# The prompt attention of a hybrid decoder: where the second 512 keys of the next step's scores stand in the order of work

## The reference, cut to what matters

```
logits = einsum(q, k_sel) * hd**-0.5          # 8 query heads, 2 KV heads, hd 64
logits = where(valid, logits, -inf)
p = softmax(logits, axis=-1)
o = einsum(p, v_sel)
```

## Time and profile before

| | us |
|---|---|
| median of 3 runs (lowest, highest) | 3653.49 (3647.55, 3655.58) |
| the profiled execution's own time | 3684.45 |
| its span | 3682.6 |
| TensorE busy | 3211.0 (87%) |
| VectorE busy | 1595.3 (43%) |
| ScalarE busy | 1179.6 (32%) |
| prompt attention, first layer | from about 730 to 905 |
| prompt attention, second layer | from about 2512 to 2687 |

### The profile page before, as it was taken

How to read it: one execution, slowest core, us unless ns; L and a number is a source line. 1 busy time by engine, 2 the same in 40 slices (tenths; PEclk the granted TensorE clock), 3 DMA queues, 4 the chain that set the end, 5 groups by cost and what they waited for, 6 DMA issues and landing times.

```text
span 3682.6 us, 58361 instructions
## 1 busy us (share of the span) xinstructions
PE 3211.0 (87%) x20553; PEld 2739.3 (74%) x20553; DVE 1595.3 (43%) x3481; ACT 1179.6 (32%) x2077; POOL 260.1 (7%) x319
## 2 busy tenths in 40 slices
PE   3997777688889999999989877777889999999995
PEld 2994533255789999999979744334558999999995
DVE  3425568965342222322343266797633423222223
ACT  3222247755332212112131223585532321211211
POOL 1001032101100000000000101310020000000000
PEclk8997789888989999999999867898979999999997
DMA  5115034302401111111122231540151111111111
GB/s 182 40 40 201 14 105 166 109 1 79 146 29 51 42 49 46 46 46 46 41 48 45 94 133 48 166 160 7 42 166 46 35 44 47 46 44 48 46 46 47
DMA packets 275990, 261.20 MB, mean 71 GB/s; under 512 B 85512, under 2 KB 237566, under 8 KB 274512
## 3 DMA queue, kind: packets, MB, share of 16 engines
q1 hardware_dynamic: 244496, 155.76, 14.2%
q0 software_dynamic: 31312, 103.20, 8.7%
HBM read 249.33 MB, written 9.78 MB: 70 GB/s over the span
## 4 chain that ended last, share of the span: by engine, by line
PE 77%; DVE 7%; issue 7%; ACT 4%; DMA 3%; POOL 1%; DVEq 0%; ACTq 0%; another core or an unknown queue 0%; POOLq 0%; SPq 0%
PE bank L711 54%; PE bank L674 5%; PE bank L748 3%; PE bank L1079 2%; ACT arena L1413 2%; PE bank L1105 2%; DMA weights<-in_w_ada 2%; DVE arena L1899 1%; PE bank L1164 1%; PE bank L759 1%; PE bank L1127 1%; DMA arena<-in_x_sample 1%; PE bank L958 1%; PE bank L1045 1%; PE bank L821 1%
## 5 line engine op out<-in xcount | busy, mean ns | idle before, releaser
L711 PE MATMUL bank<-h_hi,w_hi 128*128 128x352 f32 x2784 | 903.9, 325 | 4.5 <-DVE w_lo L1534 4.5
L711 PE MATMUL bank<-h_lo,w_hi 128*128 128x352 f32 x2784 | 893.9, 321 | 0.0
L711 PE MATMUL bank<-h_hi,w_lo 128*128 128x352 f32 x2784 | 893.8, 321 | 0.0
L711 PEld LDWEIGHTS bank<-h_hi,w_hi 128*128 128x128 f32 x2784 | 523.4, 188 | 6.9 <-issue 5.1
L711 PEld LDWEIGHTS bank<-h_lo,w_hi 128*128 128x128 f32 x2784 | 524.4, 188 | 1.7
L711 PEld LDWEIGHTS bank<-h_hi,w_lo 128*128 128x128 f32 x2784 | 522.9, 188 | 0.0
L1534 DVE TENSOR_TENSOR w_lo<-weights,w_hi 128x1024 fp32r<-128x1024 f32 x188 | 230.3, 1225 | 611.3 <-ACT w_hi L1245 605.4
L711 PE MATMUL bank<-g_hi,w_hi 128*128 128x352 f32 x1392 | 450.6, 324 | 5.5 <-DVE arena L617 5.5
L711 PE MATMUL bank<-g_lo,w_hi 128*128 128x352 f32 x1392 | 447.3, 321 | 0.0
L711 PE MATMUL bank<-g_hi,w_lo 128*128 128x352 f32 x1392 | 446.9, 321 | 0.0
L674 PEld LDWEIGHTS bank<-arena 128*128 128x128 f32 (+4 forms) x1773 | 219.4, 156 | 231.4 <-issue 180.5
(11 more groups left out here) (330 smaller groups left out, 3757.6 us busy)
## 6 DMA issues: line engine op xcount, KB each, us to landing
weights<-in_w_ada SPq DMA_DIRECT2D x64, 512.0 KB, 7.0
weights<-in_w_gate SPq DMA_DIRECT2D x44, 512.0 KB
weights<-in_w_up SPq DMA_DIRECT2D x44, 512.0 KB, 3.7
weights<-in_w_in SPq DMA_DIRECT2D x72, 256.0 KB, 3.5
arena<-in_w_ada SPq DMA_DIRECT2D x32, 512.0 KB
weights<-in_w_down SPq DMA_DIRECT2D x32, 448.0 KB, 3.5
arena<-in_w_ada SPq DMA_DIRECT2D x8, 1024.0 KB, 18.3
weights<-in_w_down SPq DMA_DIRECT2D x16, 512.0 KB, 3.8
```

What stands on the lines that cost most here:

```text
L711: mm = pe.matmul(bank[:, 0:TC], wt[:, w], xt[:, x], start=(k + m == 0), stop=(k == n_k - 1 and m == 2))
```

## The change

`qk` and `logits` get the part as an argument. In step `p` both engines issue the first part of step `p + 1` where they issued all of it; the second part follows behind the transposes of `p` on TensorE and behind their copy on VectorE. On TensorE it stands ahead of the products with V of `p - 1`, on VectorE ahead of `heads` and `select`. The two reductions and their signal come with the last part. From step 15 on (b of the next step is 3 or less) there is no second part and nothing changes. No instruction is added or removed.

```diff
-                def qk(p):
+                def qk(p, c):
                     b, i, done = PAIRS[p]
-                    for c0 in range(0, P * (b + 1), 512):
+                    for c0 in range(512 * c, min(512 * c + 512, P * (b + 1)), 512):
...
-                qk(0)
+                for c in range(2):
+                    qk(0, c)
                 for p in range(32):
                     if p < 31:
-                        qk(p + 1)
+                        qk(p + 1, 0)
                     if p % 4 == 1 and p > 4:
                         scales(p // 4 - 1)
                     turns(p)
+                    if p < 31:
+                        qk(p + 1, 1)
                     if p:
                         pv(p - 1)
...
-                def logits(p):
+                def logits(p, part):
...
-                    if i == 0 and b > 1:
+                    if i == 0 and b > 1 and part == 0:
                         dve.wait_ge(neg_ready, l * 7 + NB - b)
-                    for c, c0 in enumerate(range(0, full, 512)):
+                    for c, c0 in list(enumerate(range(0, full, 512)))[part:part + 1]:
...
-                    for g in range(2):
+                    for g in range(2 if part == k - 1 else 0):
                         dve.tensor_reduce(...).then_inc(logits_ready, 1)
...
-                logits(0)
+                for part in range(2):
+                    logits(0, part)
                 for p in range(32):
                     if p < 31:
-                        logits(p + 1)
+                        logits(p + 1, 0)
                     if p % 4 == 0 and p:
                         reciprocals(p // 4 - 1)
                     if p % 4 == 1 and p > 4:
                         scales(p // 4 - 1)
                     turned(p)
+                    if p < 31:
+                        logits(p + 1, 1)
                     if p % 4 == 1 and p > 4:
                         heads(p // 4 - 1)
```

## The result

The changed kernel takes 3635.91 us (median of 5 runs, 3632.38 to 3637.28), the kernel before 3653.49; the ratio is 0.995, with a 95% interval of 0.9935 to 0.9964. Timed again in another job it is 0.9942 (0.9929 to 0.9956): 21.4 us by this ratio, 25.4 us by the two medians (3668.82 and 3694.19). The forecast was 3634.

A forecast was written before the change was run, and what follows sets the result against it. TensorE was taken as the bound, with 29 us of gaps in the stage. A layer gains 9.9 + 1.0 + 0.3 - 1.5 = 9.7 us, 19.4 for both, giving 3634 us from the median 3653.5; range 3624 to 3649.

The forecast's parts named there:

- The removed wait: TensorE's idle time before the second part of scores, until VectorE frees a bank: up to 0.92 to 0.94 us per step goes.
- The new chain: Loop of scores, reduction, exponentials and transposes bounds steps 3 to 14: 64.3 us instead of 74.24, 9.9 less a layer.
- D: In the loop, end of the second part's matmuls to start of the exponential: 2.08, 1.81, 1.55, 1.29 us by width.
- E: In the loop, both exponentials and the signal: 2.43, 2.25, 2.03, 1.83 us for b = 7 to 4.
- T: In the loop, transposes of the second group (g = 1): 0.95, 0.83, 0.71, 0.60 us for 8 to 5 blocks.
- C: In the loop, the second part's score matmuls on TensorE: 1.13, 0.92, 0.70, 0.49 us.
- Rival B: No change: the loop takes the whole 0.93 us, or a wait after the stage absorbs the gain; 3653 us, chance 0.10.
- rival A: The loop costs 0.4 us more in each of nine steps, VectorE's work 1.5 more a layer; 3644 us, chance 0.17.
- VectorE's order: Selection pieces and `heads` delay VectorE's first-part reads and so the second part's banks: 1.5 us a layer lost, bounds 0 and 3.
- The first steps: Steps 0 to 3, TensorE at its lower clock: second part of step 3 ends 0.3 us earlier, bounds -4 and +4.
- rival D: More gain: VectorE's work costs nothing and the higher clock comes a step earlier, 3 us more a layer; 3628 us, chance 0.06.
- Rival C: Slower: TensorE's clock falls to its lower level within steps 3 to 14; 3664 us with three such steps, chance 0.07.

The follow-up runs named there:

- The delay experiment: Three extra VectorE reductions ahead of the exponentials' signal, in both orders: on the kernel before 3692.33 us, on the changed kernel 3688.72; unedited kernel before 3694.19.
- the cut pieces: Changed kernel with VectorE's selection pieces of steps 0 to 13 cut to 128 columns: one run, 3671.93 us; kernel before 3688.91 in that job.

## Why the prediction was right, point by point

- **The removed wait** was read rightly: 0.92 us in every step, and line 1079's idle time fell from 141.4 to 53.8 (forecast: under 70).
- **The new chain** was the term that decided, and its four parts held: D 1.76 (forecast 1.81), E 2.28 (2.25), T 0.91 (0.83), C 0.92 in step 6. The delay experiment shows that this loop binds the new order and not the old one. The steps bound by it take 5.87 to 6.06, 5.07 to 5.31 and 4.46 to 4.56 us with 896, 768 and 640 keys, where 5.81, 4.99 and 4.21 were forecast. Rival B, that it takes the whole gain, fell with it; of rival A (0.4 us more for each pass) 0.06 was there in step 6 and 0.2 in the mean of the nine.
- **VectorE's order** was mis-sized: 1.5 us a layer forecast, 0.3 shown by the cut pieces.
- **The second part's banks** in the 640 group were the term left out. I had written that both are read 2.0 us after the matmuls; the terms that I gave for it (start at 777.49, then 0.69 and 0.6, from 777.33) add up to 1.45. With either figure the 1.24 us of ten transposes are too short, but I wrote that transposes of 1.2 to 1.9 us cover it "or nearly so", and put the remainder at nothing. The changed kernel in step 12:

```profile
813.23 1.13 PE L1079 MATMUL bank<-arena 64*128 64x512 f32 x4
...
814.29 1.45 PE L674 MATMUL bank<-arena 128*128 128x128 f32 x10
814.55 0.69 DVE L2022 CUSTOM_DVE_ANT_0 arena<-bank,arena 128x512 f32<-128x512 f32 x1 [0.27 <-PE bank L1079]
...
815.17 0.69 DVE L2022 CUSTOM_DVE_ANT_0 arena<-bank,arena 128x512 f32<-128x512 f32 x1
...
815.91 0.49 PE L1079 MATMUL bank<-arena 64*128 64x128 f32 x4 [0.18 <-DVE arena L2022]
```

  The first part ends at 814.36; the second can start 1.55 later, and ten transposes fill 1.24. That step takes 4.56 where the sum had 4.21, and it stays at 4.56 with the selection pieces cut. This and T's 0.07 to 0.1 a step make up most of what VectorE's order did not cost: the twelve steps sum to 66.05 against 64.3 + 1.5 = 65.8. That these two errors cancelled was luck.
- **The end** held: ten transposes of step 14 already done gave 1.24 (from the end of the last second part to step 16's first part it was 2.42 us and is 1.18), and step 15's wait for its exponentials took 0.35, where 0.2 was forecast. That leaves 0.9 against 1.0.
- **The first steps** were the mis-sized term of the total: 0.3 us forecast, within bounds of 4, and 2.5 us measured, since I had laid them out at the lower clock to step 2. This is why a layer gains 11.6 us up to step 17 (8.2 + 0.9 + 2.5) and not 9.7. It comes close to rival D, which had 3 us more for a layer: D's two causes, VectorE's order at nearly nothing and an earlier rise of the clock, were both there, and only the bank wait and T of the points above took part of it back.
- **Rival C**, the clock falling on the new idle time, did not happen. Scores of 512 columns stay at 1.13 us from step 2 on, although TensorE now stands up to 0.49 us before the first group of transposes and some 0.25 between the two. The Trainium skill (TensorE: Matmul & The Clock Gate, "A second HAM failure mode: psum-queue depth-cycling") tells of a kernel in which short idle spells between groups of matmuls made the clock swing. The trace doesn't agree with this here: from step 2 to step 16 no such spell brought the 1.13 us to 2.08.
- **Nothing else moves** holds as far as step 22: the steps from 16 on have their lengths, and the gain stands at 23 us for both layers. The timed comparisons have 17.6 us, and 21.4 by the ratio of the repeat, with intervals of 13 to 24 and 16 to 26 us (the interval's ends by the median before). Behind step 22 the traces differ by more than the order: from the first scores to the last `scales` of a layer the kernel before took 173.4 and 173.2 us in one trace and 175.9 and 173.1 in the other, the changed kernel 157.6 twice and 160.5 twice.
- **The total** is nearer than the working deserves. The stage gained 23 us where 19.4 were forecast, and the first timed comparison gave 17.6: the distance of 2 us between 3634 and 3635.9 is smaller than either difference, and so partly luck.

What stays open: whether the difference between 23 and 17.6 us is only the spread of the runs or a loss behind the stage, where the clock's lower level and the stop in step 23 fall differently from trace to trace; no experiment was made for it.

## What to carry to other kernels

When a wait on a buffer is filled by moving other work into it, add up the loop that the move closes (here scores, reduction, exponential, transposes) and compare it with the busy engine's own work in a step; the larger one is the new step. Then the same sum tells the next edit: signalling the first half of a result ahead of the second took nothing off the stretch in the old order and gave 8 us in the new one. A helper piece that is moved on one engine has to be followed into the queues of the engines that wait for it.

## What the runs showed of the hardware

The same program differs by up to 1.1% between jobs (3653 to 3694 us). The traces show one place of it: in some, TensorE, VectorE and ScalarE stop in step 23, while GpSimd goes on issuing its gathers. In the first trace of the kernel before VectorE stood 5.42 us although its bank was full, ScalarE 6.7 and TensorE 2.4:

```profile
877.07 0.69 DVE L2053 CUSTOM_DVE_ANT_0 weights<-bank,weights 128x512 f32<-128x512 f32 x1 [5.42 <-remote]
```

In the changed kernel's first trace, from a quicker job, the stop is absent; in its second it is back with 6.9 us. The traffic of the gathers doesn't tell the two apart: the DMA engines were busy nine tenths of the time or more both during the stop and in the same steps of the trace without it. What causes the stop wasn't tried.

The clock can fall without idle time. In the kernel before TensorE was busy 16.25 of these 17.00 us, with small transposes, products of few columns and 32-row bf16 masks, and the granted clock was 0.68:

```profile
888.00:905.00 17.00, 16.25 (x92) 8.11 (x93) 8.56 (x41) 8.35 (x33) 0.00 (x0) 0.68 0.08 29
```

In the changed kernel the fall itself stands behind full work: TensorE was busy for the whole of 864 to 870 us at a granted clock of 1.00, and then, still without idle time:

```profile
870.00:872.00 2.00, 2.00 (x12) 0.71 (x8) 1.04 (x5) 1.07 (x5) 0.00 (x0) 0.75 0.03 8
872.00:874.00 2.00, 2.00 (x13) 1.05 (x11) 1.10 (x9) 1.26 (x6) 0.00 (x0) 0.50 0.00 0
```

TensorE's share of busy time in the profile is thus no sufficient sign of the level that it is granted.
